# Squares summed on TensorE, a reciprocal moved behind C22, an earlier query split, and a regrouped start of the input projection in a two-layer streaming encoder

## What is computed

```
for l in 0, 1:
    x += 0.5 * SwiGLU(RMSNorm(x))          # first half FFN, hidden 2816
    z  = RMSNorm(x) @ w_in                 # 16 chunks of 128 columns
    groups A (chunk-band MHA), B (latent attention), C (window GQA, sinks)
    x += concat(o_a, o_b, o_c) @ w_out
    x += 0.5 * SwiGLU(RMSNorm(x))          # second half FFN
y = RMSNorm(x)
RMSNorm(x) = x * rsqrt(mean(x*x) + 1e-6) * g
# group B: q = RMSNorm(z_cq) @ w_uq  (rank 384, "latent queries"); keys and values from a latent of rank 256
```

## Time and profile before

| | |
|---|---|
| median of 3 runs | 2131.88 us (2124.45 to 2136.68) |
| the profiled execution | 2132.1 us |
| its span, first to last instruction | 2130.3 us |
| mean granted TensorE clock | 0.988 of full speed |
| PE busy | 2037.2 us, 96% of the span |
| DVE, ACT, POOL busy | 69%, 47%, 27% |
| DMA | 206.86 MB, mean 97 GB/s |

### The profile page before, as it was taken

How to read it: one execution, slowest core, us unless ns; L and a number is a source line. 1 busy time by engine, 2 the same in 40 slices (tenths; PEclk the granted TensorE clock), 3 DMA queues, 4 the chain that set the end, 5 groups by cost and what they waited for, 6 DMA issues and landing times. The chain is left out here.

```text
span 2130.3 us, 42670 instructions
## 1 busy us (share of the span) xinstructions
PE 2037.2 (96%) x15802; PEld 1940.9 (91%) x15802; DVE 1472.8 (69%) x2559; ACT 994.2 (47%) x2064; POOL 582.5 (27%) x481
## 2 busy tenths in 40 slices
PE   6999999999999899999989999999999999999996
PEld 5999999997678899999989999999967789999996
DVE  7984896443766986697788659754456578838953
ACT  5552553323654673354457325532255456625542
POOL 4420341211432440242134024212042333303411
PEclk9999999999999999999999999999999999999998
DMA  3233234532000234223322423334310013332241
GB/s 137 95 123 120 80 100 158 185 103 73 11 21 31 80 98 158 80 99 120 118 80 98 150 72 104 131 125 183 107 36 1 31 41 99 128 119 90 99 150 52
DMA packets 58868, 206.86 MB, mean 97 GB/s; under 512 B 6809, under 2 KB 8729, under 8 KB 58201
## 3 DMA queue, kind: packets, MB, share of 16 engines
q1 hardware_dynamic: 51840, 186.80, 26.0%
q10 hardware_dynamic: 6884, 18.10, 2.2%
HBM read 198.06 MB, written 7.41 MB: 96 GB/s over the span
## 5 line engine op out<-in xcount | busy, mean ns | idle before, releaser
L1229 DVE SCALAR_TENSOR_TENSOR w_lo<-raw,w_hi 128x512 fp32r<-128x512 f32 (+2 forms) x306 | 335.4, 1100 | 196.3 <-ACT w_hi L688 196.0
L688 ACT ACTIVATE w_hi<-raw 128x512 fp32r<-128x512 f32 (+2 forms) x306 | 222.5, 733 | 215.2 <-PE banks L1712 177.1
L1738 PE MATMUL banks<-xg_hi,w_hi 128*128 128x272 f32 x1008 | 292.7, 290 | 18.6 <-DVE w_lo L1229 15.0
L1143 POOL TENSOR_TENSOR w_sum<-raw 128x512 f32<-128x512 f32 x84 | 123.9, 1475 | 668.5 <-PE banks L1738 334.1
L1738 PE MATMUL banks<-xg_hi,w_lo 128*128 128x272 f32 x1008 | 292.9, 291 | 0.0
L1738 PE MATMUL banks<-xg_lo,w_hi 128*128 128x272 f32 x1008 | 291.4, 289 | 0.0
L1738 PEld LDWEIGHTS banks<-xg_hi,w_hi 128*128 128x128 f32 x1008 | 190.8, 189 | 21.9 <-DVE w_lo L1229 11.0
L1738 PE MATMUL banks<-t_hi,w_hi 128*128 128x272 f32 x672 | 194.9, 290 | 9.9 <-DVE w_lo L1229 8.5
L1738 PE MATMUL banks<-t_hi,v_hi 128*128 128x272 f32 x672 | 196.5, 292 | 8.1 <-ACT u L738 4.5
L1738 PE MATMUL banks<-t_hi,w_lo 128*128 128x272 f32 x672 | 194.9, 290 | 0.0
L1738 PE MATMUL banks<-t_hi,v_lo 128*128 128x272 f32 x672 | 194.6, 290 | 0.0
(11 more groups left out here) (222 smaller groups left out, 5377.5 us busy)
## 6 DMA issues: line engine op xcount, KB each, us to landing
raw<-w_stream SPq DMA_DIRECT2D x352, 512.0 KB, 3.8
mla_quv<-w_mla ACTq DMA_DIRECT2D x2, 2048.0 KB, 12.0
bias<-bias_in ACTq DMA_DIRECT2D x2, 1698.5 KB, 6.8
x<-x_in ACTq DMA_DIRECT2D x4, 272.0 KB, 6.8
x<-x_in SPq DMA_DIRECT2D x4, 272.0 KB, 7.4
av_out<-vt ACTq DMA_DIRECT2D x2, 544.0 KB, 2.8
ak_out<-ak ACTq DMA_DIRECT2D x2, 544.0 KB, 4.1
ckv_out<-ckv ACTq DMA_DIRECT2D x2, 544.0 KB, 3.3
```

The source lines that it names most:

```text
L688: nc.scalar.activation(hi, from_, ACT.Copy).then_inc(hi_split, 1)
L1143: done = nc.gpsimd.tensor_tensor(total, a21, a22, ALU.add)
L1229: nc.vector.scalar_tensor_tensor(lo, from_, 1.0, hi.bitcast(f32), ALU.mult, ALU.subtract).then_inc(lo_split, 1)
L1738: done = mm(banks[:, bank, 0:HALF], w[:, wk], v[k], start=fresh and k == 0 and step == 0, stop=k == KD // 2 - 1 and step == 2, skip_group_ ...
```

## The change

On PE: the first norm's squares are no longer added by POOL but by PE, each square tile multiplied by the ones matrix and accumulated in PSUM (`add_squares`): four tiles after the whole pair, four after p6 of pair 1. In the projection, jobs 0 and 1 are done together: the first seven tiles of job 0, the first seven of job 1, then the last tile of each, then the sum. At the end, PE multiplies `sqacc` (seven tiles) ahead of the last square and adds that square by a second accumulating product, which takes POOL's last addition away.

On DVE: in all openings, not only the first, the reciprocal moves from before C11 of pair 1 to behind C22 and the low part of S4 of pair 2, and both scales follow it; pairs 1 and 2 are written out ahead of the loop, which turns 3 times in place of 4. At the end, five of the six products for y read the factor from PSUM (`pair(1)`), where ACT has copied it.

On ACT: in every up cycle the high part of S4 is made before the copy of p1's result, not after; the bases b_first of the first sums are made between the first tiles of x in place of after them; parking in the first opening comes earlier; the split of the latent queries and the Exp table load move from the start of the attention into the projection, behind the prep `value_rows` 1.

```diff
+        SQUARES = (sqacc[:, :], sq[:, :], early[:, 0, :], early[:, 1, :], gate[:, :])
...
             def up_cycle(l, p, n, i=0, tile=None):
...
+                make_hi(l, ("up", p, n + 1, "S4"), i)
                 copy_s1(l, p, n + 1, i)
-                make_hi(l, ("up", p, n + 1, "S4"), i)
...
+                if 1 <= m <= KD // 2:
+                    nc.scalar.activation(b_first[:, m - 1, :], x[:, m - 1, :], ACT.Copy, scale=gain0[:, m - 1:m]).then_inc(b_set, 1)
...
+                        if (kind, c) == ("value_rows", 1):
+                            act.wait_ge(tab_set, nth(tab_set, l, 1))
+                            act.wait_ge(zq_gained, nth(zq_gained, l, KQ))
+                            nc.scalar.activation(zq_hi[:, :, :], zq[:, :, :], ACT.Copy).then_inc(zq_hi_set, 1)
+                            nc.scalar.activation(spare[:, :], epsb[:, :], ACT.Exp)
...
-                act.wait_ge(tab_set, nth(tab_set, l, 1))
-                nc.scalar.activation(zq_hi[:, :, :], zq[:, :, :], ACT.Copy).then_inc(zq_hi_set, 1)
...
+            act.wait_ge(rstd_set, DEPTH * NORMS + 1)
+            nc.scalar.activation(pair(1), halves(rstd[:, :]), ACT.Copy).then_inc(rstd_copied, 1)
...
-                    if opens_all(l, p):
-                        first_sums(range(1, 4))
...
-                if not opens_all(l, p):
-                    reciprocal_root(l, N_UP2 if p else N_UP1)
                 read_c11(l, p, 1, 0)
-                if not opens_all(l, p):
-                    scale_c11(l, p, 1, 0)
...
-                if opens_all(l, p):
-                    up_cycle(l, p, 1, first_norm=N_UP1)
-                    up_cycle(l, p, 2)
+                up_cycle(l, p, 1, first_norm=N_UP2 if p else N_UP1)
+                up_cycle(l, p, 2)
...
             def first_win_jobs(l):
 
                 pe.wait_ge(result_read, nth(result_read, l, J_WIN - 1))
-                win_job(l, 0, 0, N_WIN)
+                for tiles in (ORDER[:KD - 1], ORDER[KD - 1:]):
+                    for c in range(2):
+                        made(l, ("win", c))
+                        for k in tiles:
+                            pe.wait_ge(xg_set, nth(xg_set, l, tile_count(N_WIN, k)))
+                            done = tile_products(c, ("win", c), k, xg_hi[:, k, :], xg_lo[:, k, :], k == ORDER[0], k == ORDER[KD - 1])
+                        if k == ORDER[KD - 1]:
+                            done.then_inc(chunk_used, 1)
                 pe.wait_ge(sq_sum, nth(sq_sum, l, N_WIN * KD))
                 pe.wait_ge(result_read, nth(result_read, l, J_WIN))
                 sum_of(sqacc, 3).then_inc(norm_summed, 1)
-                win_job(l, 1, 1)
                 win_job(l, 2, 2)
...
+            def add_squares(l, tiles):
+
+                pe.wait_ge(const_loaded, 16)
+                for j in tiles:
+                    pe.wait_ge(sq_one, j + 1)
+                    acc = SQUARES[j % len(SQUARES)]
+                    for half, done in ((0, None), (1, norm_summed if j == KD - 1 else sq_sum)):
+                        added = mm(banks[:, 2 * SUM_PAIR + half, 0:HALF], ones, acc[:, half * HALF:(half + 1) * HALF],
+                                   start=j == 0, stop=j == KD - 1, skip_group_check=True)
+                        if done is not None:
+                            added.then_inc(done, 1)
```

More of the change, by code:

```diff
@@ L428, in encoder_program @@
         with ExitStack() as a:
+            uq_hi = [sb("uq_hi0", [P, KQ, P], f32r, a)]
+            sb("behind_uq_hi0", [P, T - KQ * P], f32, a)
             zq_hi = sb("zq_hi", [P, KQ, T], f32r, a)
[L430 removed]
+            uq_hi.append(sb("uq_hi1", [P, KQ, P], f32r, a))
         sb("place_of_rstd", [P, 5 * T])
[L432 removed]
+        assert KQ * P <= T and KQ * (T + P) <= 4 * T
         consts = sb("consts", [P, CONSTS])
@@ L764, in first_square, with open_cycles @@
             def first_square(j):
[L766 to L791, removed]
-                make_hi(l, ("up", p, 2, "A12"))
-                make_hi(l, ("up", p, 2, "S1"))
-                copy_u2(l, p, 1, 0)
+                if j >= len(SQUARES):
+                    act.wait_ge(sq_sum, j + 1 - len(SQUARES))
+                nc.scalar.activation(SQUARES[j % len(SQUARES)], x[:, j, :], ACT.Square).then_inc(sq_one, 1)
+            def open_cycles(l, p):
                 make_hi(l, ("up", p, 2, "S2"))
@@ L809, in open_all @@
                 up_cycle(l, p, 2)
+            def open_all(l, p):
+                count_whole()
+                bulk_hi(l, 0, 0, t1_made, t1_hi_set)
+                make_hi(l, ("up", p, 1, "A11"))
+                make_hi(l, ("up", p, 1, "S1"))
+                for j in range(4):
+                    first_square(j)
+                park(l, p, WHOLE_BANKS)
+                bulk_hi(l, 0, 1, t2_made, t2_hi_set)
+                make_hi(l, ("up", p, 1, "A12"))
+                copy_s1(l, p, 1, 0, True)
+                make_hi(l, ("up", p, 1, "S4"))
+                make_hi(l, ("up", p, 1, "S2"))
+                copy_p5(l, p, 1, 0, True)
+                bulk_hi(l, 0, slice(2, 4), t4_made, t34_hi_set)
+                make_hi(l, ("up", p, 1, "S3"))
+                make_hi(l, ("up", p, 2, "A11"))
+                for j in range(4, KD):
+                    first_square(j)
+                make_hi(l, ("up", p, 1, "A22"))
+                make_hi(l, ("up", p, 2, "A12"))
+                make_hi(l, ("up", p, 2, "S1"))
+                copy_u2(l, p, 1, 0)
+                open_cycles(l, p)
             def bulk_hi(l, which, t, made, done):
@@ L1029, in _ @@
                     make_hi(0, first[1])
+                if 1 <= m <= KD // 2:
+                    nc.scalar.activation(b_first[:, m - 1, :], x[:, m - 1, :], ACT.Copy, scale=gain0[:, m - 1:m]).then_inc(b_set, 1)
             make_hi(0, first[2])
             make_hi(0, first[3])
-            for m in range(KD // 2):
-                nc.scalar.activation(b_first[:, m, :], x[:, m, :], ACT.Copy, scale=gain0[:, m:m + 1]).then_inc(b_set, 1)
             for dst, old in rolls:
@@ L1170, in ffn @@
                     norm(l, N_UP2)
-            def first_sums(tiles):
-                places = (None, sq[:, :], early[:, 0, :], early[:, 1, :], gate[:, :], sq[:, :], early[:, 0, :], early[:, 1, :])
-                for j in tiles:
-                    pool.wait_ge(sq_one, j)
-                    pool.wait_ge(sq_sum, j)
-                    nc.gpsimd.tensor_tensor(sqacc[:, :], sqacc[:, :], places[j], ALU.add).then_inc(sq_sum, 1)
             def norm(l, k):
-                for j in range(1, KD):
+                for j in range(1, KD - int(l == DEPTH - 1 and k == N_UP2)):
                     pool.wait_ge(sq_one, nth(sq_one, l, k * (KD - 1) + j))
@@ L1839, in up_open @@
                 if opens_all(l, p):
-                    pe.wait_ge(parked_read, nth(parked_read, l, which + 1))
-                    up_cycle(l, p, 1, first_norm=norm)
+                    add_squares(l, range(4, KD))
+                    up_cycle(l, p, 1)
                     up_cycle(l, p, 2)
```

50 lines of the change are left out of this document (26 added, 24 removed).

## The result

| | before | changed |
|---|---|---|
| median (lowest to highest) | 2129.55 us (2124.45 to 2136.68), 5 runs | 2119.48 us (2117.55 to 2120.56), 5 runs |
| ratio of the two | | 0.9945, 95% interval 0.9926 to 0.9964 |
| span of the profiled execution | 2130.3 us | 2117.7 us |

The change gains half a per cent: the time lies inside the forecast range, 3.5 us above the forecast. Part of that closeness is luck. The forecast's sum starts from 2132.1 us, the median of the five runs before is 2129.55, and the gain between the medians is 10.1 us where 16.1 were forecast. A later set of runs gave 0.9961 (0.9947 to 0.9975).

A forecast was written before the change was run, and what follows sets the result against it. PE, busy 96% of 2130.3 us, bounds the kernel: time is won or lost where it stands or runs below full clock. -9 - 10 + 15.4 - 8.5 - 4 = -16.1 from 2132.1 gives 2116.0 us, range 2104 to 2126.

The forecast's parts named there:

- Term 3: Start of the projection: regrouping delays job 2 by 6.0 us a layer, plus clock loss; +15.4 us, bounds +12 and +19.
- Term 1: First opening: PE's waits for DVE go, eight sums on PE replace one; -9 us, bounds -5 and -12.
- I add 1 for the waits between them: First opening: 1 us allowed for remaining waits on top of the 28 us that both bounds gave.
- The signs named for the term: First opening's timeline: PE waits under 3 us in all, eight float32 sums, p1 of pair 3 near 52 us.
- Term 2: Three other openings: waits for low parts behind the reciprocal go, with some clock; -10 us, bounds -6 and -11.5.
- 0 to 0.5 us each would come back: Three other openings: cost of the later reciprocal, for which C11's and C12's scales and pair 1's gate wait.
- Term 4: Attention's start: waits for the first exponentials and the clock loss behind them go; -8.5 us, bounds -3 and -9.
- term 5: The end: POOL's last addition goes, the sum is split, products read PSUM; -4 us, bounds -1.3 and -4.6.
- (a): Rival: DVE stays the bound of the openings, whose gains would be -4 and -5 us; 2126 us, chance 0.13.
- (b): Rival: no hole in the projection, ACT's and DVE's splits run ahead, cost about 0; 2100.6 us, chance 0.05.
- (c): Rival: clock stays at 1.2 GHz behind the projection's hole, each job 5.99 us longer; slower than 2142.8 us, chance 0.04.
- (d): Rival: other hidden waits replace those at attention's start and end, gains -3 and -1.3 us; 2124.2 us, chance 0.10.

The follow-up runs named there:

- e2: The kernel before with the regrouped start of the projection alone: 2140.79 us, ratio 1.0070 to the kernel before.
- e1: The changed kernel with the projection's old start (job 0 whole, sum, job 1): 2103.44 us, ratio 0.9891 to the kernel before.
- e4: The changed kernel run again as it is, in a later set: 2119.90 us, ratio 0.9961 to the kernel before.
- e6: The changed kernel with POOL adding the first norm's squares again, early parking and bases kept: 2125.22 us, ratio 0.9976 to the kernel before.
- e5: The changed kernel with the reciprocal and C11's scale back before pair 1's C11 in the three other openings: 2126.77 us, ratio 0.9979.
- e7: The changed kernel with a reciprocal of one column in place of 544 in the FFNs' four openings: 2112.00 us, ratio 0.9912.
- e10: The changed kernel with the end's six products reading the factor from SBUF, no ACT copy, sum still in two parts: 2121.34 us, ratio 0.9963.
- e9: The changed kernel with the whole old end (POOL's last addition, one sum, products reading SBUF): 2123.72 us, ratio 0.9974.
- e11: The changed kernel, regrouped start kept, with chunk 2 split ahead of the root, DMA issues and reciprocal: 2105.05 us, ratio 0.9887.
- e8: The changed kernel with the latent queries' split and Exp table load back at the attention's start: 2131.07 us, ratio 0.9999.
- e3: The changed kernel with the projection's old start and chunk 2 split ahead of the norm's chain: 2097.88 us, ratio 0.9859.

## Why the prediction was right, and where its terms were off

The direction and the signs of all five terms were right, and the forecast of 2116.0 was 3.5 us low. In the two profiled executions the terms' errors are +2.4, +3.1, -1.6, -0.6 and -0.5 us. They partly cancel: the two that the change was made for were too large, and the forecast gain of 16.1 us was 10 us in one set of runs and 7.5 in the other.

**Term 3, the projection (+15.4, measured +13.8; 13.4 by e2, 16.5 by e1 against e4).** The step that a chain of 9.05 us no longer has job 1's 6.0 us in it is shown by e1, e2 and by 9.08 us in the changed trace. The clock's share was laid on both layers alike. In layer 0 it was -0.4: PE works at half clock for 3.4 us there before and for 2.8 after. In layer 1 it was +2.2: none before, 5.0 us at half clock after. The 2.8 us are the least of eighteen; in most of the others layer 0 had 4.3 to 6.1 us, and the term comes nearer to the forecast.

**Term 1, the first opening (-9, measured -6.6).** The contention was right (e6), and so was the price of a square, 0.92 us. The step that failed is "I add 1 for the waits between them". The waits are 1.54 for the low part of a token sum, 1.67 for ACT's fifth square and 1.50 for `make_hidden`: 4.7 us. The third I had in my own rows and let go with the others, though its releaser, a DVE operation that reads PSUM, was another than theirs. The first has its counterpart in the trace before, in a row that the prediction did not count:

```profile
37.70 0.36 PE L1738 MATMUL banks<-t_hi,w_hi 128*128 128x272 f32 x1 [1.15 <-DVE t_lo L1258]
```

How much the kernel before loses in this opening differs from execution to execution, too (58.06 us in e2), so the term's true size is known only to some 4 us. The signs named for the term came short: waits of 4.7 us in place of under 3, and p1 of pair 3 at 54.5 us in place of 52.

**Term 2, the other openings (-10, measured -6.9, and -3.7 to -6.0 in the other eight traces).** This is the term that was furthest off. All three waits went, as forecast (and e5 brings them back). Of the clock, the 1.7 us of layer 0 went as counted. The step that failed is "0 to 0.5 us each would come back": it was too low, and the sum took nearly none of it. What came back is 0.63 + 0.68 us (p7 and p4 of pair 2) in both second FFNs, and 1.17 + 0.63 + 0.40 in layer 1's first, where only 0.8 us was won. e7 prices all that the reciprocal still costs in the four openings at 7.5 us, a comparison across sets. I had said who waits for it (scales and gate) but did not follow them to the PSUM bank that p1 of pair 3 needs.

**Term 4, the attention (-8.5, measured -9.1) and term 5, the end (-4, measured -4.5)** held in both their parts. In term 5 the shares were a little off: 2.4 and 1.4 by e10 and e9, for 2.1 and 1.8. With the whole old end (e9) the stretch is 20.2 us, and 19.9 in e2, where the sum ran at full clock; 20.9 in the trace before is thus on the long side, and the part is worth 3.4 to 4.5.

**The rivals.** (a), DVE stays the bound of the openings: its sign, more than 15 us of waits there, did not come. A small part of it, the reciprocal holding pair 3 back, did. (b), no hole: refuted, 8.00 and 7.84 us. Only e11 makes the hole vanish, and by another change. (c), the clock stays down: refuted; it was back within 5.0 us, and within 6.1 in all eighteen cases. (d), other waits in their place at attention and end: refuted by e8 to e10.

Left open: why PE runs at half clock somewhere in the attention in some executions, with the same program. In four of thirteen traces it lengthens one layer to over 150 us.

## What to carry to other kernels

When a matmul job stands between the start of a norm's chain and its consumer, it is paid cover: count the chain (sum, root, DMA issues, split) from end to end before moving the sum behind it, since here 9.05 us stayed 9.05 and the job's 6 us were added. Look first for what in the chain the next job really needs: chunk 2's split needed nothing of the norm, and put ahead of root, issues and reciprocal it was worth 6 us, and 15 with the regrouped order. An operation moved off one consumer's path lands on another's: follow it up to the PSUM bank it keeps.

## What was not expected of the hardware

- After every wait of about 8 us in front of job 2 (nine kernels, two layers each) PE ran at half clock for 2.8 to 6.1 us. After 1.6 to 2.0 us it was not settled: 3.4 us at half clock in layer 0 of the kernel before and none in layer 1, none in layer 0 of e1 and a window of 0.83 in layer 1, none in either layer of e11.

```profile
410.00:420.00 10.00, 10.00 (x83) 10.00 (x81) 5.92 (x5) 3.84 (x5) 7.54 (x5) 1.00 0.98 397
...
1440.00:1450.00 10.00, 8.21 (x54) 8.00 (x53) 5.62 (x5) 4.17 (x5) 4.39 (x3) 0.83 1.01 402
```

  These are windows of e1 around the two waits, PEclk being the third number from the right.
- The stretch from the waiting uq product to the second norm's sum is the same program in all kernels; it took 147.7 to 149.4 us in 22 of 26 cases and 150.3 to 151.6 in four, with no wait to show for it, only a lower granted clock.
- In e3 the nine DMA issues on ACT took 6.25 us in place of 4.75, single ones up to 1.40 us, though they are the same issues and only began 6.7 us earlier in the program's time. It cost nothing there.
